# Pairing attention units on ScalarE, splitting two softmax steps, and moving lookups and closings in a one-core block kernel

## What is computed

```python
xn = rmsnorm(h, ln)
qa, ka, va, qb, kb, vb = split(xn @ w_in)
# group A, 8 heads, for each block of 128 queries against all earlier keys:
z = q_i @ k_i.T * scale
log_fail = where(s < t, -softplus(z), 0)
later_fail = cumsum(log_fail, reverse=True) - log_fail
o_a = where(s < t, exp(log_sigmoid(z) + later_fail), 0) @ v_i
# group B, 8 heads over 2 kv heads: rotary, own chunk + previous chunk + meta tokens,
o_b = softmax(concat(scores, sink))[..., :-1] @ v
h = h + concat(rmsnorm(o_a), rmsnorm(o_b)) @ w_out
# experts, for each token t and 8 heads:
q = rmsnorm(h) @ w_query                       # two halves of 64
s1, i1 = top_k(half 0 . keys, 16); s2, i2 = top_k(half 1 . keys, 16)
top_s, idx = top_k(all sums s1 + s2, 16)       # 128 experts a token
g = softmax(top_s)
act = gelu(expert_u[idx] . x_t)
h = h + sum(g * act * expert_v[idx])
out = rmsnorm(h) * final_norm
```

## Time and profile before

| | |
|---|---|
| profiled execution | 2905.47 us |
| its span | 2903.7 us, 32738 instructions |
| TensorE products | 2349.3 us busy, 81% |
| VectorE | 2214.9 us, 76% |
| ScalarE | 1253.3 us, 43% |
| GpSimd | 1363.3 us, 47% |
| indirect gathers | 1026.06 MB, 87.0% of sixteen DMA engines |
| all DMA | 389 GB/s on average |
| blocks 3, 4, 5, 6 | from 1262, 1598, 1918 and 2223 us; block 7 from 2551 us |

### The profile page before, as it was taken

How to read it: one execution, slowest core, us unless ns; L and a number is a source line. 1 busy time by engine, 2 the same in 40 slices (tenths; PEclk the granted TensorE clock), 3 DMA queues, 4 the chain that set the end, 5 groups by cost and what they waited for, 6 DMA issues and landing times.

```text
span 2903.7 us, 32738 instructions
## 1 busy us (share of the span) xinstructions
PE 2349.3 (81%) x9955; PEld 1049.4 (36%) x9955; DVE 2214.9 (76%) x5454; ACT 1253.3 (43%) x3127; POOL 1363.3 (47%) x1126
## 2 busy tenths in 40 slices
PE   9988888788887888867887788868756779977897
PEld 7564532345333453313421242213311233333332
DVE  4189886786767877679788869878788756899845
ACT  3523377432653235633475447834332432322223
POOL 0024354444554445544565455655555544444442
PEclk9999999999999999979898898978977889987899
DMA  8279999999999999999999999999999999999998
GB/s 317 100 314 413 382 412 419 402 416 389 407 383 416 409 402 404 392 420 420 421 414 418 349 389 382 377 404 391 412 401 402 387 412 413 393 421 386 420 420 347
DMA packets 199519, 1130.54 MB, mean 389 GB/s; under 512 B 29735, under 2 KB 51431, under 8 KB 73719
## 3 DMA queue, kind: packets, MB, share of 16 engines
q0 software_dynamic: 147456, 1026.06, 87.0%
q1 hardware_dynamic: 51888, 102.38, 9.4%
HBM read 1158.08 MB, written 18.02 MB: 405 GB/s over the span
## 4 chain that ended last, share of the span: by engine, by line
PE 37%; DVE 24%; DMA 18%; ACT 11%; issue 8%; POOL 2%; ACTq 0%; POOLq 0%; DVEq 0%; SPq 0%
DMA r_uv<-in_experts,r_wk 18%; PE ps L2285 15%; DVE r_uv L1759 8%; PE ps L1887 4%; PE ps L2069 3%; PE ps L2188 3%; PE ps L2166 2%; ACT L1214 2%; ACT r_uv L1226 2%; PE ps L1881 2%; PE ps L2033 1%; DVE r_wk L1417 1%; DVE r_wk L1419 1%; DVE r_wk L1420 1%; ACT L951 1%
## 5 line engine op out<-in xcount | busy, mean ns | idle before, releaser
L2285 PE MATMUL ps<-r_uv 128*64 128x512 f32 x4096 | 1167.2, 700 | 526.6 <-ACT r_uv L1226 523.0
L930 POOL DMA_INDIRECT r_uv<-in_experts,r_wk x640 | 771.5, 1205 | 920.8 <-PE ps L2285 776.2
L1759 DVE CUSTOM_DVE_ANT_0 r_uv<-r_uv,hnrep 128x1024 f32<-128x1024 f32 x640 | 782.9, 1242 | 312.4 <-DMA r_uv<-in_experts,r_wk 307.3
L2285 PEld LDWEIGHTS ps<-r_uv 128*64 128x64 f32 x4096 | 280.6, 151 | 1173.0 <-ACT r_uv L1226 703.9
L925 POOL DMA_INDIRECT r_uv<-in_experts,r_wk x384 | 494.8, 1289 | 437.6 <-PE ps L2285 314.8
L1214 ACT ACTIVATE r_wk<-r_wk 128x2 f32<-128x2 f32 x512 | 103.8, 203 | 1286.9 <-DVE r_wk L1759 1285.1
L1759 DVE CUSTOM_DVE_ANT_0 stream_chunk<-r_uv,hnrep 128x1024 f32<-128x1024 f32 x192 | 238.5, 1242 | 88.7 <-DMA r_uv<-in_experts,r_wk 88.5
L1759 DVE CUSTOM_DVE_ANT_0 stage<-r_uv,hnrep 128x1024 f32<-128x1024 f32 x192 | 236.0, 1229 | 60.8 <-DMA r_uv<-in_experts,r_wk 57.1
L1226 ACT ACTIVATE r_uv<-cst,r_wk 128x64 f32<-128x64 f32 x634 | 186.0, 340 | 10.3
L1214 ACT ACT_TABLE_LOAD x135 | 173.2, 1283 | 2.4
L951 ACT ACT_TABLE_LOAD x115 | 147.5, 1283 | 12.1 <-PE ps L2146 8.1
(11 more groups left out here) (236 smaller groups left out, 2776.9 us busy)
## 6 DMA issues: line engine op xcount, KB each, us to landing
r_uv<-in_experts,r_wk POOLq DMA_INDIRECT x1024, 11.3
stream_chunk<-in_w_chunks SPq DMA_DIRECT2D x30, 512.0 KB, 8.1
r_wk<-lkv_dram SPq DMA_DIRECT2D x36, 256.0 KB, 8.2
r_wo<-in_dense_u SPq DMA_DIRECT2D x16, 512.0 KB, 7.9
r_wo<-in_experts SPq DMA_DIRECT2D x16, 512.0 KB, 8.0
r_uv<-in_x SPq DMA_DIRECT2D x8, 512.0 KB, 10.7
r_wo<-in_w_chunks SPq DMA_DIRECT2D x8, 512.0 KB, 11.5
r_wk<-in_x SPq DMA_DIRECT2D x8, 512.0 KB, 7.8
```

The source lines that it names most:

```text
L930: g.indirect_dma_start(uv[:, SLOT[G], :], None, experts, bass.IndirectOffsetOnAxis(idx[b % 2][:, k:k + 1], 0)).then_inc(rows_in[SLOT[G]], 16)
L1759: v.tensor_tensor_reduce(spent[k % 2] if b in DENSE else uv[:, slot, 0:D], uv[:, slot, 0:D], hnrep[:, k % GRP, :], 1.0, 0.0, ALU.mult, ALU ...
L2285: last = t_.matmul(ps[HALF * j:HALF * j + HALF, i, :], uv[:, slot, 0:HALF], uv[:, slot, D + 512 * i:D + 512 * i + 512], start=n == 0, stop ...
```

## The change

Four edits. (1) In blocks 3 and 4 logs and weights of units with an even number stand one group later, so that both units of a pair stand in one group, with weights of the pair before ahead of them; scores of these blocks take turns in five PSUM banks, the fifth being bank 7 (the edits that only pass `late_bank` along are left out of the diff). (2) In blocks 5 and 6 "exp" is split into heads 0 to 3 in group 6 and heads 4 to 7 in group 7, "mask" into "added" in group 4 and "most" in group 5; in block 6 "norm" and "pT" with all that follows up to the mixing stand one group later, "h2" stays. (3) In block 4 lookups of heads 5, 6 and 7 stand in groups 9, 11 and 13 instead of 3, 10 and 12, "gate" in 19 instead of 18. (4) In block 7 each closed tile gets its own root and scale, two groups after its sum, instead of one root and three scales in groups 61 and 62.

```diff
--- before.py
+++ after.py
+LATE_BANKS = {0: Z_BANKS, 1: Z_BANKS, 3: Z_BANKS + (7,)}
...
+
+
+def logs_at(first, u):
+
+    return LATE_AT[first][u] + LOGS + (first == 3 and u % 2 == 0)
+
+
+def weights_at(first, u):
+
+    return LATE_AT[first][u] + WEIGHTS[first] + (first == 3 and u % 2 == 0)
+
+
+def units_at(at, first, group):
+
+    return [u for u in range(len(LATE_AT[first])) if at(first, u) == group]
...
-CLOSE_SQUARE_AT, CLOSE_SCALE_AT, CLOSE_GAIN_AT = max(CLOSE_ADD_AT) + 1, max(CLOSE_ADD_AT) + 2, min(CLOSE_ADD_AT)
+CLOSE_GAIN_AT = min(CLOSE_ADD_AT)
...
                     a.activation(se, se, ACT.Exp).then_inc(exp_ready, 1)
+                elif step[0] == "soft":
+                    if step[1] == 0:
+                        act.wait_ge(max_ready, t + 1)
+                    for h in range(4 * step[1], 4 * step[1] + 4):
+                        last = a.activation(ssb[:, h, :], ssb[:, h, :], ACT.Exp, bias=nmx[:, h:h + 1], accum_out=rs[:, h:h + 1])
+                    if step[1]:
+                        a.activation(se, se, ACT.Exp).then_inc(exp_ready, 1)
                 elif step == "pT":
...
-            at_5 = {6: "exp", 10: "pT", 12: "ob", 13: "oa", 16: "r2", 20: "h2sq", 23: "hnT", 28: ("qT", 0),
+            at_5 = {6: ("soft", 0), 7: ("soft", 1), 10: "pT", 12: "ob", 13: "oa", 16: "r2", 20: "h2sq", 23: "hnT", 28: ("qT", 0),
...
-            at_6 = {6: "exp", 9: "pT", 11: "ob", 12: "oa", 14: "r2", 18: "h2sq", 21: "hnT", 26: ("qT", 0),
+            at_6 = {6: ("soft", 0), 7: ("soft", 1), 10: "pT", 12: "ob", 13: "oa", 15: "r2", 18: "h2sq", 21: "hnT", 26: ("qT", 0),
...
-                link(a.activation(qT_v[:, :], closing[i], ACT.Square, accum_out=close_sums[:, i:i + 1]))
-
-            def close_roots():
-                rsqrt_mean(close_roots_of, close_sums, D).then_inc(close_squared, 1)
+                link(a.activation(qT_v[:, :], closing[i], ACT.Square, accum_out=rs[:, 2 * i:2 * i + 1]))
+                rsqrt_mean(rs[:, 2 * i + 1:2 * i + 2], rs[:, 2 * i:2 * i + 1], D).then_inc(close_squared, 1)
...
-                    if b == NT - 1 and n == CLOSE_SQUARE_AT:
-                        close_roots()
-                    if late is not None and (late_units(late, n - WEIGHTS[late]) or late_units(late, n - LOGS)):
+                    if late is not None and (units_at(weights_at, late, n) or units_at(logs_at, late, n)):
...
-                        for u in late_units(late, n - WEIGHTS[late]):
+                        for u in units_at(weights_at, late, n):
...
-                        for u in late_units(late, n - LOGS):
+                        for u in units_at(logs_at, late, n):
...
                 elif step == "mask":
+                    tile_step("added", t)
+                    tile_step("most", t)
+                elif step == "added":
                     dve.wait_ge(score_done, t + 1)
...
                     link(last)
+                elif step == "most":
                     link(v.tensor_reduce(mx, ssb[:, :, :], AX.X, ALU.max))
...
-            at_5 = {2: "rope", 5: "mask", 8: "norm", 10: "pT", 17: "r2", 19: "h2", 21: "hn", 37: ("scores", 0), 38: ("numbers", 0),
+            at_5 = {2: "rope", 4: "added", 5: "most", 8: "norm", 10: "pT", 17: "r2", 19: "h2", 21: "hn", 37: ("scores", 0), 38: ("numbers", 0),
...
-            at_6 = {2: "rope", 5: "mask", 7: "norm", 9: "pT", 15: "r2", 17: "h2", 19: "hn", 35: ("scores", 0), 36: ("numbers", 0),
+            at_6 = {2: "rope", 4: "added", 5: "most", 8: "norm", 10: "pT", 16: "r2", 17: "h2", 19: "hn", 35: ("scores", 0), 36: ("numbers", 0),
...
-            own_of = [own_first, at_own, at_own, at_own, own_late, own_5, own_late, own_late]
+            own_4 = {9: [("pick", 5)], 11: [("pick", 6)], 13: [("pick", 7)], 19: [("gate", 1)], 22: [("routed", 1)]}
+            own_of = [own_first, at_own, at_own, at_own, own_4, own_5, own_late, own_late]
...
-            def close_scale():
-
-                dve.wait_ge(close_squared, 1)
+            def close_scale(i):
+
+                dve.wait_ge(close_squared, i + 1)
...
-                m, q = rden[:, 0:ND], rden[:, ND:2 * ND]
-                v.tensor_scalar(m, close_sums, 1.0 / D, EPS, ALU.mult, ALU.add)
-                link(v.tensor_tensor(q, close_roots_of, close_roots_of, ALU.mult))
-                link(v.tensor_tensor(q, q, m, ALU.mult))
-                link(v.tensor_scalar(q, q, -0.5, 1.5, ALU.mult, ALU.add))
-                link(v.tensor_tensor(close_roots_of, close_roots_of, q, ALU.mult))
-                for i in range(ND):
-                    hg = grid(closing[i], 2)
-                    v.scalar_tensor_tensor(out=hg, in0=hg, scalar=close_roots_of[:, i:i + 1], in1=ps[:, 2:4, :], op0=ALU.mult,
-                                           op1=ALU.mult).then_inc(close_ready, 1)
+                polish(rs[:, 2 * i + 1:2 * i + 2], rs[:, 2 * i:2 * i + 1], D)
+                hg = grid(closing[i], 2)
+                v.scalar_tensor_tensor(out=hg, in0=hg, scalar=rs[:, 2 * i + 1:2 * i + 2], in1=ps[:, 2:4, :], op0=ALU.mult,
+                                       op1=ALU.mult).then_inc(close_ready, 1)
...
                             close_add(CLOSE_ADD_AT[n])
-                        if n == CLOSE_SCALE_AT:
-                            close_scale()
+                        if n - 2 in CLOSE_ADD_AT:
+                            close_scale(CLOSE_ADD_AT[n - 2])
                     if n == (9 if later_gain else 7 if b else 12) and b < NT - 1:
...
-                            if n == LATE_AT[late][last_of(late, i)] + WEIGHTS[late] + 2:
+                            if n == weights_at(late, last_of(late, i)) + 2:
...
-                    if u < ZB:
+                    zb = len(LATE_BANKS[first])
+                    if u < zb:
...
-                                            (key_kept, 4 * b + 8))[u]
+                                            (key_kept, 4 * b + 8), (key_kept, 4 * b + 8))[u]
...
-                    if u >= ZB:
-
-                        gate(pe, "pe", lw_ready, ub + u - ZB + 1)
+                    if u >= zb:
+
+                        gate(pe, "pe", lw_ready, ub + u - zb + 1)
...
-                unit_scores(u, h, h == 0, r, c0, lkv[m][:, P * (j % 2):P * (j % 2) + P], lq[:, i % 2, :])
+                unit_scores(u, h, h == 0, late_bank(first, u, r, c0), c0, r, lkv[m][:, P * (j % 2):P * (j % 2) + P], lq[:, i % 2, :])
...
-            at_6 = {1: ["turn"], 3: ["scores"], 8: ["pT"], 10: ["pv", halves[0]], 11: halves[1:3], 12: halves[3:4], 13: ["ssq", halves[4]],
-                    14: halves[5:7], 15: halves[7:8], 18: ["gain"], 20: ["hnT"], 31: [("keys", 1)]}
+            at_6 = {1: ["turn"], 3: ["scores"], 9: ["pT"], 11: ["pv", halves[0]], 12: halves[1:3], 13: halves[3:4], 14: ["ssq", halves[4]],
+                    15: halves[5:7], 16: halves[7:8], 18: ["gain"], 20: ["hnT"], 31: [("keys", 1)]}
...
-                        for u in late_units(late, n - WEIGHTS[late] - 1):
+                        for u in units_at(weights_at, late, n - 1):
```

31 lines of the change are left out of this document (18 added, 13 removed).

## The result

Timed in turn on one chip, the changed kernel took 2950.78 us (median of 4 runs, 2947.84 to 2953.06), the kernel before 2911.92 (2905.36 to 2917.47): ratio 1.0136, 95% interval 1.0113 to 1.0158, some 39 us. The forecast was 2921, slower, with 2937 as the upper end: the direction held, and the change cost 2.7 times what was forecast. The two profiled executions lie further apart than the medians, 2950.0 against 2903.7 us of span.

The account below looks back on a forecast made before the run. No single limit: the gather queue bounds late block 3, a ScalarE-TensorE loop late block 4. Terms 4 + 12 - 3.5 + 0 + 1.5 + 0.5 = +14.5 us gave 2921 us; range 2898 to 2937, leaving out 2 in 10.

Parts of the forecast that it names:

- Late block 4: Groups 32 to 59: the ScalarE-TensorE loop over three groups grows from 14.4 to 15.84 us; +12 us, bounds -1 and +16.
- The term for the clock: Late block 4: one gap of nearly 4 us may put TensorE at half rate, 1.5 us each time; 0.5 us added.
- each loop starts at half rate: Rival, blocks 3 and 4: first groups slow, block 4 stage 149 us, +14 there, +8 in block 3, 2927 us; chance 0.08.
- "even" rival: Rival, late block 4: TensorE stays at the high clock, stage 135.5 against 134.9 us, whole 2906 us; chance 0.31.
- The 1.4: Late block 4: us added per loop by pairing, 15.84 against 14.4, over eight full loops 11.5 us.
- Late block 3: Groups 32 to 59: loop mean 16.4 us against the DMA's 15.7 costs 6, partly covered by queued requests; +4, bounds 0 and +9.
- The rival of the freed loads: Rival, late blocks 3 and 4: ScalarE's saved table loads count in full until DMA limits, -12 and -1, 2892 us; chance 0.16.
- VectorE's wait for logs: Late blocks: softplus gets logs one group later, but has about 10 us per loop with nothing else queued in that order.
- Early block 4: Lookups moved to groups 9, 11 and 13 let mask and mixing start 3.9 us earlier; -3.5 us, bounds -5 and 0.
- Block 5: Softmax in halves, where only ScalarE's halves and "added" move: 0 us, bounds -2 and +3.
- Block 6: Softmax in halves puts 4 us of table loads and gelu ahead of the norm; +1.5 us, bounds -2 and +5.
- Closings: Block 7's end: fewer last scales, against a scale delaying group 61's dots by 2.1 us; +0.5, bounds -1.5 and +2.5.

Follow-up runs that it names:

- the run that removed most of VectorE's wait: The changed kernel with VectorE's softplus of the even units one group later: 2950.64 us, ratio 1.0133 to the kernel before.
- the other edits alone: The changed kernel without the pairs and the fifth bank (lookups, softmax halves and closings remain): 2912.69 us, ratio 0.9999 to the kernel before.
- turning two neighbours round: The kernel before, unpaired, with ScalarE's logs put ahead of the weights: 2906.01 us, ratio 0.9971 to the kernel before.
- with ten: The changed kernel with each odd unit's first score product done ten times more in late blocks 3 and 4: 2946.6 us, ratio 1.0103.
- the unpaired kernel: The kernel before with logs ahead of weights and the change's block 4 lookups: 2904.61 us, ratio 0.9968; with four added products per late unit: 2909.73 us, 0.999.

## Why the prediction was wrong

**Late block 4, +12 forecast, +15.4 measured: mechanism right, clock mis-sized.** The loop was rebuilt to the step, and the run that removed most of VectorE's wait leaves no more than a few microseconds to it. The term for the clock, "I add 0.5 us in all, bounds 0 and 9 x 0.9", is wrong: 8 of the groups were slow against 4 before, and the loops read in the trace run at 17.4, 1.5 above the sum. The rival "each loop starts at half rate", to which I gave a chance of 0.08, has 149 us for the stage, within the 148.0 to 153.3 of the same code. That +12 came near is in part luck. The forecast and the "even" rival both start from 15.84, and one adds 8 x 1.4 to the measured stage while the other has 9 x 15.84 - 7 = 135.5. The 1.4 compares two loops at the high clock, but the 134.9 that it is added to holds loops of 16.0 with a slow first group, so slow groups were in the +12 without being in its clock term. I had the gap of "nearly 4" in hand, and priced it from the two rows at 2.16 and 2.35 us. In the changed kernel's late block 4 TensorE has eight rests of 2.6 to 4.7 us, and the groups behind all eight take 3.15 to 3.68. The "even" rival, at 0.31, needed the high clock throughout and was far off, although a loop that had it took 15.50. The advice of the Trainium skill (TensorE: Matmul & The Clock Gate, "Why this matters for your kernels") against long idle gaps between bursts is borne out here, 8 of 27 groups against 4, and was worth more than I gave it; but rests of 3.3 us went both ways on the same code, so it is no certainty.

**Late block 3, +4 forecast, +18.4 measured: the step that failed.** The 16.4 us per loop were set against a DMA need of 15.7. At 17.3 the DMA covers nothing (its share fell to 0.94), which makes it +8. On top of that come the sums' copy and the lookup, 4 to 6 us together, and a part that no run names. The part on the change named the gelu and the softplus as queued behind the waits, and never the copy, whose place in the program follows the weights' (`+ 2`) and so moved with them. It stands in VectorE's queue ahead of a lookup and of two dots, in a block where VectorE was busy 124.8 of 141.1 us.

**The rival of the freed loads (0.16).** Half of the loads went, all 24 us of them, and the time rose, so ScalarE's total was not the bound. The Trainium skill (ScalarE: Activation LUTs, "Table sets: the hidden batching unit") has the work grouped by table set; the loads were saved as it says, but the grouping put two units' work behind one wait. Between loads and activations there is still no drain, 0.02 us at 1806.14 + 1.28 to 1807.44.

**VectorE's wait for logs.** The text said that softplus has room. It does wait, 20 us a stage, so the reading was wrong; but in eight of the nine loops of late block 4 that wait is off the chain, and taking most of it away did not shorten the stage.

**Early block 4, -3.5: held.** -3.9 in the changed kernel, -4.5 with the other edits alone; twelve profiles with the new places lie at 92.6 to 95.9, four with the old at 97.2 to 99.8.

**Block 5, 0 forecast, +7.7 measured: failed.** I costed the halves on ScalarE and wrote "only ScalarE's halves and 'added' move". "Added" is an instruction that waits for TensorE, and moving it one group up put group 5's dots behind that wait, which was the question to ask. The upper bound of +3 for this stage was too low by the same omission.

**Block 6, +1.5 forecast, +7.6 measured.** With the mask in group 5 it is 2.1 (125.9 against 123.8), the forecast's own size; the norm's wait came out at 5.4 us, near the 5 that were written. The rest goes with "added" again, but the addition's own wait is 1.0 us, so the cause stays open.

**Closings, +0.5: held**, 0.6 over the block, though the stretch from the issue of the last gather to the end grew by 2.4 us (23.8 to 26.2), where "within 1 us" was written.

Added up, the forecast's terms came to 14.5 and the stages to 45.8. Of the miss of 31 us the mask is 12 (6.2 and 5.5, by one profile), the halves 2, the clock 3 in block 4, the slower loops against the DMA's need 4 in block 3, copy and lookup 4 to 6, and the last 4 to 6 us of block 3 have no name.

## What to carry to other kernels

When two engines hand work to each other in a loop, busy time saved on one counts only if it lies on the loop; here 24 us less of ScalarE in a stage came with 15 us more of time, and turning two neighbours round (the step whose input is ready first, ahead of the one that waits) gave some 8 us in the whole, 2 to 15 by its interval, for nothing. Of a step that is moved to an earlier place, ask first whether it waits, and what stands behind it; of a step whose place is computed from another's, follow it too. A rest ahead of a burst is priced from rests of its length, not from shorter ones.

## What the runs showed that I had not expected

Small products in TensorE's rest brought the clock back: with ten, slow groups in late block 4 fell from 8 to 1. No single length of rest decides it: in late block 3 of the kernel before a group behind 3.27 us took 1.94. Yet in the unpaired kernel the same cure, with the slow groups down to 2 and 0, was worth nothing. A slow group was seen to cost time where the next step waited for its end. And the stretch of blocks 0 to 2, the same code in every kernel, took between 1084.2 and 1096.4 us over these profiles, so that differences of a few us in a whole time say little, while stages cut at the same groups can be compared.
